# Moving the weight rings and gated outputs of a two-block transformer kernel 64 bytes further on in on-chip memory

## The reference, cut to what matters

```python
def first_block(x, mem, ...):
    for i in range(DEPTH):                      # 2 layers
        if i % 2 == 0:
            x = x + even_mixer(rmsnorm(x, e_norm[j]), e_w_in[j], e_sink[j], e_w_out[j])
        else:
            x = x + conv_mixer(rmsnorm(x, o_norm[j]), o_w_in[j], ...)
        x = x + memory_cross_attention(rmsnorm(x, c_norm[i]), rmsnorm(mem, c_mem_norm[i]),
                                       c_wq[i], c_wkv[i], c_wo[i])
    return rmsnorm(x, final_norm)

def second_block(x, mem, ...):
    proj = rms_norm(x, mix_norm_g) @ w_in       # pooling, latent attention, memory attention, gates
    merged = gates[0] * (y_pool @ w_br_pool) + gates[1] * (y_mla @ w_br_mla) + gates[2] * (y_mem @ w_br_mem)
    x = x + merged @ w_out
    x = x + hierarchical_moe(rms_norm(x, ffn_norm_g), ...)   # 32 experts, 2 of them for each token
    return rms_norm(x, final_norm_g)
```

## Time and profile before

| | |
|---|---|
| time, median of 3 runs | 1642.08 us (1639.98 to 1642.35) |
| span of the profiled execution, first to last instruction | 1635.1 us |
| PE busy | 1594.2 us, 7432 products |
| DVE, ACT, POOL busy | 844.8, 583.8, 547.7 us |
| mean granted TensorE clock | 0.991 of full speed |

### The profile page before, as it was taken

One profiled execution on the slowest core, in us unless ns is written; L12 is line 12 of the kernel. 1 busy time (PEld: TensorE's weight loads), 2 busy tenths in 40 slices (PEclk: granted clock), 3 DMA queues, 4 the chain that ended last, 5 costly groups with the idle time before them and its releaser, 6 DMA issues.

```text
span 1635.1 us, 20099 instructions
## 1 busy us (share of the span) xinstructions
PE 1594.2 (97%) x7432; PEld 1203.1 (74%) x7432; DVE 844.8 (52%) x1456; ACT 583.8 (36%) x963; POOL 547.7 (33%) x239
## 2 busy tenths in 40 slices
PE   7999989999999999999999999999999999999997
PEld 5888768886888888887877667888877885444543
DVE  5448577125655546354668687343242544443434
ACT  4127544334332225324533342343243333112213
POOL 4441226731444444751334123455424410000000
PEclk9999999999999999999999999999999999999998
DMA  5331224521332323441222113334222349999992
GB/s 187 92 102 39 78 78 124 160 90 60 100 92 91 102 91 98 160 128 40 80 77 69 40 48 94 114 110 136 91 64 91 117 191 356 418 422 421 423 417 82
DMA packets 52787, 235.94 MB, mean 144 GB/s; under 512 B 6240, under 2 KB 7136, under 8 KB 48096
## 3 DMA queue, kind: packets, MB, share of 16 engines
q1 hardware_dynamic: 48960, 222.60, 38.8%
q0 software_dynamic: 2016, 7.34, 1.1%
q10 hardware_dynamic: 1728, 4.87, 0.9%
HBM read 230.59 MB, written 4.19 MB: 144 GB/s over the span
## 4 chain that ended last, share of the span: by engine, by line
PE 90%; DVE 6%; issue 2%; ACT 1%; DMA 0%; SPq 0%; DVEq 0%; ACTq 0%
PE G L1802 69%; PE O L1802 7%; PE S L1802 6%; PE TR L1802 4%; PE TR L1912 2%; DVE sumsq L994 1%; PE G L2374 1%; DVE sq L1054 1%; DMA w_ring<-in_stream_dram 0%; ACT hi_ring L570 0%; DVE U L1025 0%; DVE sumsq L1124 0%; DVE arena L1424 0%; DVE U L1779 0%; DVE arena L1203 0%
## 5 line engine op out<-in xcount | busy, mean ns | idle before, releaser
L535 POOL TENSOR_TENSOR lo_ring<-w_ring,hi_ring 128x1024 fp32r<-128x1024 f32 x219 | 534.0, 2440 | 788.0 <-ACT hi_ring L570 787.7
L570 ACT ACTIVATE hi_ring<-w_ring 128x1024 fp32r<-128x1024 f32 x219 | 231.3, 1059 | 587.4 <-PE G L1802 583.1
L1802 PE MATMUL G<-xa_hi,hi_ring 128*128 128x512 f32 x928 | 378.8, 408 | 9.8 <-DVE xa_lo L1116 9.7
L1802 PE MATMUL G<-xa_hi,lo_ring 128*128 128x512 f32 x928 | 364.9, 393 | 0.0
L1802 PE MATMUL G<-xa_lo,hi_ring 128*128 128x512 f32 x928 | 363.1, 391 | 0.0
L1802 PEld LDWEIGHTS G<-xa_hi,hi_ring 128*128 128x128 f32 x928 | 175.1, 189 | 48.6 <-issue 12.3
L1802 PEld LDWEIGHTS G<-xa_lo,hi_ring 128*128 128x128 f32 x928 | 175.1, 189 | 40.3 <-issue 2.6
L1802 PEld LDWEIGHTS G<-xa_hi,lo_ring 128*128 128x128 f32 x928 | 174.8, 188 | 39.8
L1802 PE MATMUL G<-yb_hi,hi_ring 128*128 128x512 f32 x388 | 154.4, 398 | 3.4 <-ACT arena L668 2.2
L1802 PE MATMUL G<-yb_hi,lo_ring 128*128 128x512 f32 x388 | 151.6, 391 | 0.0
L1802 PE MATMUL G<-yb_lo,hi_ring 128*128 128x512 f32 x388 | 151.4, 390 | 0.0
(11 more groups left out here) (350 smaller groups left out, 2501.4 us busy)
## 6 DMA issues: line engine op xcount, KB each, us to landing
w_ring<-in_stream_dram SPq DMA_DIRECT2D x219, 512.0 KB, 3.5
arena<-in_w_gu_dram SPq DMA_DIRECT2D x16, 2048.0 KB, 11.9
ex_rings<-in_w_dn_dram SPq DMA_DIRECT2D x40, 512.0 KB, 15.8
ex_low<-in_w_gu_dram SPq DMA_DIRECT2D x8, 2048.0 KB, 18.4
ex_rings<-in_w_gu_dram SPq DMA_DIRECT2D x8, 2048.0 KB, 16.0
arena<-in_w_dn_dram SPq DMA_DIRECT2D x16, 512.0 KB, 14.4
sq<-in_w_dn_dram SPq DMA_DIRECT2D x8, 512.0 KB, 18.1
X<-in_x_in_dram SPq DMA_DIRECT2D x8, 256.0 KB, 6.2
```

Of the source, the lines that this page charges most:

```text
L535: nc.gpsimd.tensor_tensor(lo_ring[:, s, :], w_ring[:, s, :], hi_ring[:, s, :], ALU.subtract).then_inc(low, 1)
L570: nc.scalar.activation(hi_ring[:, m % RING, :], w_ring[:, m % RING, :], ACT.Copy).then_inc(high, 1)
L1802: return nc.tensor.matmul(*args, **kw)
```

## The change

One tensor of 64 bytes, `line_b`, is asked for behind the small ones. Nothing reads or writes it. It puts everything behind it 64 bytes further on: `w_ring` from 159,040 to 159,104, `hi_ring` from 171,328 to 171,392, `lo_ring` from 183,616 to 183,680, `yb_lo` from 195,904 to 195,968, `yb_hi` from 212,288 to 212,352, and `ex_rings`, `ex_low` and `ex_raw` with them. All of these then begin on a multiple of 128 bytes, as the large tensors ahead of them already did. The instructions of every engine, their order and their waits are the same, one by one.

```diff
--- before.py
+++ after.py
@@ -40,6 +40,7 @@
 QUADS = EXPERTS // 4
 ROUNDS = T // SLOTS
 SUMMED = KT - 2
+HALF_LINE = 16
@@ -148,6 +149,7 @@
         snk = sb("snk", [P, 4, 2])
         esnk = sb("esnk", [P, 4, 2])
         rcp = sb("rcp", [P, 4, 2])
+        sb("line_b", [P, HALF_LINE])
         before_experts = ExitStack()
```

## The result

The changed kernel takes 1624.31 us, median of five runs (1623.14 to 1626.2), against 1641.57 us for the kernel before, median of five (1638.08 to 1642.35). The ratio is 0.9908, interval 0.9891 to 0.9924: some 17 us faster. The prediction said 8.5 us, its time 1633.6 and its range 1629 to 1646, so the direction was right, the size was half of what came, and the time lies outside the range.

A forecast was written before the change was run, and what follows sets the result against it. PE, busy 1594.2 of 1635.1 us, was taken as the bound. Pace terms summed to 10.5 us, cut to 8.5, giving 1626.6 us profiled; the 7 us offset carried over made 1633.6 us, range 1629 to 1646.

The forecast's parts named there:

- `xa` and `cm` of 512 columns: 2940 PE products of xa and cm against the rings, from 228.9 to 226.7 ns each: 6.5 us gained.
- ring moving: 384 PE products with the ring as moving operand, from 233.4 to 226.7 ns each: 2.6 us gained.
- `scatter`: 256 PE products in the experts' stage, taken at the difference of 233.4 to 226.7 ns: 1.7 us gained.
- `yb`: About 400 yb products in single or half tiles, 228.8 to 226.7 ns: 0.8 us gained; long runs nothing.
- 256 columns: 480 PE products of 256 columns, from 117.8 to 120.0 ns each: a loss of 1.1 us.
- off for breaks and the tenth not PE's: A tenth of the chain is not PE's, 10.5 to 9.5 us; streams restarting after breaks take another 1 us.
- The pace of 512 columns at (0, 0): Both operands on multiples of 128 bytes: taken as 226.7 ns a product, bounds 213.3 and 233.4.
- Rivals 1, 2 and 3: 1: remainder irrelevant, 1642 us, 0.20; 2: aligned pairs settle slow, 1661 us, 0.14; 3: aligned start saves line, 1570 us, 0.05.
- the rings' other readers and writers: POOL and ACT on the rings: POOL would have to become twice as slow to matter; nothing in both directions.
- stand 7 us above it ... which I carry over: Timed runs, median 1642.08 us, stand 7 us above the profiled 1635.1; added to 1626.6 to give 1633.6 us.
- Keep step on the memory when they begin alike: Moving and next stationary operand with equal remainders to 128 cost their own lines and exactly one more.
- halves of 13.33 ns: 128 bytes pass in 13.33 ns; halves of that step come in where the operands' remainders differ by 64 bytes.

The follow-up runs named there:

- c_before: The kernel before, run once more without any edit: 1641.49 us, ratio 1.0003, span 1639.6 us.
- all_64: Against the kernel before: 64 bytes ahead of everything plus the change's 64 bytes, so all large tensors begin 64 behind a multiple of 128; 1624.59 us, ratio 0.9900.
- swap: Against the kernel before: 64 bytes ahead of everything, without the change's 64, so rings begin at 0 and other large tensors at 64; 1640.70 us, ratio 0.9998.
- cm_eq: Against the kernel before: cm alone moved 192 bytes, everything behind it 256, so only cm is at distance 0 from the rings modulo 256; 1631.54 us, ratio 0.9945.
- after_cm: The changed kernel with cm put back to distance 64 from the rings, everything behind it 256 bytes further; 1630.12 us, ratio 0.9945 to the kernel before.
- nudge: Kernel before, addresses unchanged, one tiny ACT instruction ahead of one unit's hi_ring in each of the two memory stages, making POOL later; 1635.97 us, ratio 0.9970.
- cm_64: Against the kernel before: cm moved 64 bytes and tensors behind it another 64, so the rings moved 128; 1640.67 us, ratio 0.9999.
- pad_192: Kernel before with line_b of 192 bytes instead of the change's 64, putting xa and cm 128 from the rings modulo 256; 1641.45 us, ratio 1.0012.
- pad_128: Kernel before with line_b of 128 bytes instead of the change's 64, putting xa and cm 192 from the rings modulo 256; 1646.79 us, ratio 1.0053.
- c_after: The changed kernel run once more in the last set: 1625.75 us, ratio 0.9908 to the kernel before.

## Why the prediction was wrong in size

**The account.** Between the spans of `c_before` and of the changed kernel lie 1639.6 - 1622.5 = 17.1 us. I measured the pace terms as mean start distances over all products of a kind, in both traces. The two waits give 3.1. The clock gives (1 - 0.988) x 1639.6 - (1 - 0.991) x 1622.5 = 5.1 us in this pair, by rounded means, so within some 1.6 us; by the means over runs it is some 3 us. Together with the paces that is 8.6 + 3.1 + 5.1 = 16.8 of the 17.1 us. Since the products are the same in both traces, one by one, they can also be laid side by side: 3.1 us for the two waits, 5.5 for the steps in stretches at the half clock, 8.9 for the paces, and -0.4 for other pauses. Only 1.5 of the 5.5 us stand right behind a wait. `c_before` lost 3.2 and 1.6 us in stretches at 25 and 220 us, ahead of both waits, which the changed kernel's execution happened not to have; `all_64`, just as quick on the median, has stretches at 212 and 861 us. So the clock term of this pair is in good part the luck of two executions.

| term | predicted us | measured us |
|---|---|---|
| `xa` and `cm` of 512 columns | 6.5 | 6.1 (229.4 to 227.3 ns) |
| ring moving | 2.6 | 2.3 (233.3 to 227.2) |
| `scatter` | 1.7 | 0.5 (233.5 to 231.4) |
| `yb` | 0.8 | 0.65 (227.6 to 227.0) |
| 256 columns | -1.1 | -0.96 (117.8 to 119.85) |
| off for breaks and the tenth not PE's | -2.0 | not seen as such |
| the paces together | 8.5 | 8.6 |
| two waits at the memory norms | 0 | 3.1 |
| stretches at the half clock | 0 | 5.1 in this pair, some 3 on the mean |

**The pace of 512 columns at (0, 0)**, the one unknown that was bounded between 213.3 and 233.4 ns, was taken as 226.7 and came as 226.7. Rivals 1, 2 and 3 fall with it. The Trainium skill's N / 2.4 + 2.5 ns (page "TensorE: Matmul & The Clock Gate", section "Back-to-back issue gap"), some 216 as an estimate, was reached nowhere. The page gives it for a product by itself, without a weight load of its own. The fastest steady pace of any pair of operands here is 226.7.

**Luck in the sum of the paces.** 8.5 predicted and 8.6 measured agree better than the terms do. They were predicted at 10.5 in full and came to 8.6: `scatter` was over-sized by 1.2 us, since it does not reach 226.7, and the others by some 0.7 together. The 2 us taken off for other reasons happened to cover that.

**The step that failed** is the part on the rings' other readers and writers and what it left unsaid. It asked whether POOL could become late for PE, found that it would have to be twice as slow, and wrote "I put this at nothing in both directions". That holds for POOL against PE (`swap`). It did not ask whom POOL's start makes late: DVE, in the one place where PE waits for a sum. The 256-column term was booked as a loss of 1.1 us, and `cm_eq`, `after_cm` and `nudge` show that it is the term whose side effect is worth several times its cost: 3.1 us of waits, and with the clock 5.1 us in `nudge`. The half clock had no term in the sum at all; it came to some 5 us in this pair of executions and some 3 us on the mean. The 256-column pace moves POOL's start by 2.2 ns x 24 = 0.05 us a unit, and 0.06 us was what POOL was ahead. It could have been read in the trace of the kernel before, though none of the rows shown has it: the two POOL and DVE instructions start next to each other, and DVE's 2.9 us for 512 columns is out of line with its 0.68 elsewhere.

**A second weakness** is the time made out of the span: "stand 7 us above it ... which I carry over". With 1.8 us as the offset and a typical span of 1639 the base is the same median, but the comparison of the profiled spans (12.6 us) hides 4.5 us of the gain. This did not make the 8.5 wrong; it hid that the profiled execution had less of the half clock (0.991) than the usual run (0.989), and that there was something to gain there.

**What was right for a reason that is too narrow.** "Keep step on the memory when they begin alike" was worked out from remainders to 128. By it `cm_64` should not have hurt `xa`, and `pad_192` should have been as fast as the change. The halves of 13.33 ns do not hold either: 116.2 and 119.3 ns are 8.7 and 8.95 of them. The condition seen here, for products against the rings, is the difference modulo 256. Whether the memory explains it was argued and is not shown.

**Open.** Why distances of 64 and 192 differ is not settled, nor why the moving ring at 64 has two paces in `pad_128`, nor why `scatter` at 0 stays near 231, nor why `xa` at 64 runs for long stretches at 228.9 and in others at 233.4. That waits bring half-clock stretches rests on a count of six in fourteen against none in fourteen; what rule decides which of them do, and why the means of the clock differ by more than twice what these stretches explain, is not known. No kernel here beat the changed one; `all_64` and `c_after` equal it.

## What to carry to other kernels

In long streams of `float32r` products of 512 columns with a weight load each, place the moving and the stationary operand at the same address modulo 256 bytes; where both are is indifferent. With 256 columns it is the other way round, by up to 4 ns. Then ask not only what a new pace does to PE, but which two instructions of other engines start within a tenth of a microsecond of each other, and which of them goes first afterwards: some 0.1 us on POOL's start was worth 5.1 us in `nudge`, against the 6.1 that the pace of 2940 products brought. And take the span from several executions before a term of 8 us is set against it.

## What the runs showed of the hardware that I had not expected

- A distance of 32, 128 or 192 bytes costs a 512-column product 6.2 to 6.6 ns against equal starts, one of 64 only 2.2 to 3.4; with 256 columns equal starts are the slowest (119.9 to 120.0), and a distance of 192 is the fastest (116.2).
- A DVE addition of two operands in on-chip memory takes 0.68 us when it starts first and 2.87 behind a POOL subtraction of 2.38 us that started 0.06 us earlier. When DVE is first by 0.03 us, the POOL subtraction takes 2.90 us.
- The granted clock fell to 0.50 for 3.3 us although PE was fully busy in that stretch, 1.4 us behind a wait of 1.39 us. Such a stretch began 1.3 to 2.4 us behind six of fourteen such waits, and behind none of fourteen such sums without one.
